# A hybrid decoder layer on one core: a new order for the modulation's weight loads, with the gate rows kept in DRAM

## The reference

```python
mod = silu(c) @ w_ada + b_ada                 # w_ada is 2048 x 12288
sh1, sc1, gt1, sh2, sc2, gt2 = split(mod, 6)
h = rms_norm(x, g_pre_mix) * (1 + sc1) + sh1
u_lru, u_gate, q, k, v, f_logit = split(h @ w_in, ...)
y_lru = rg_lru(conv4(u_lru), ...) * gelu(u_gate)
y_att = fox_attention(q, k, v, cumsum(log_sigmoid(f_logit + b_forget)))     # 8 heads of 128
y = concat(rms_norm(y_lru, g_lru_out), rms_norm(y_att, g_att_out)) @ w_out
x = x + gt1 * rms_norm(y, g_post_mix)
h = rms_norm(x, g_pre_mlp) * (1 + sc2) + sh2
x = x + gt2 * rms_norm(relu(h @ w_ff1) ** 2 @ w_ff2, g_post_mlp)
```

## Time and profile before

| | us |
|---|---|
| median of 3 runs (lowest, highest) | 2317.61 (2315.52, 2321.9) |
| the profiled execution | 2320.91 |
| span of its trace, first to last instruction | 2319.1 |
| PE busy in it | 2150.2 (93%) |
| DVE busy in it | 1627.2 (70%) |
| ACT busy in it | 800.6 (35%) |
| granted TensorE clock, mean | 0.965 of full speed |

### The profile page before, as it was taken

How to read it: one execution, slowest core, us unless ns; L and a number is a source line. 1 busy time by engine, 2 the same in 40 slices (tenths; PEclk the granted TensorE clock), 3 DMA queues, 4 the chain that set the end, 5 groups by cost and what they waited for, 6 DMA issues and landing times.

```text
span 2319.1 us, 25157 instructions
## 1 busy us (share of the span) xinstructions
PE 2150.2 (93%) x9081; PEld 1707.6 (74%) x9081; DVE 1627.2 (70%) x1783; ACT 800.6 (35%) x1032; POOL 159.2 (7%) x140
## 2 busy tenths in 40 slices
PE   4779999999888896699999999999999999999996
PEld 3557778888666675477877877877787787787775
DVE  7998694456774755577677677668668667767756
ACT  4224622222542233234333334333333333333332
POOL 3440040000110001000000000000000000000000
PEclk7789999999999998799999999999999999999998
DMA  9865466647326762433232333232232322323242
GB/s 331 291 223 161 139 193 192 187 121 264 110 87 199 256 207 95 159 101 109 82 118 90 99 99 109 81 118 90 90 112 96 99 99 99 101 89 108 100 150 105
DMA packets 178574, 322.45 MB, mean 139 GB/s; under 512 B 12328, under 2 KB 47256, under 8 KB 176336
## 3 DMA queue, kind: packets, MB, share of 16 engines
q1 hardware_dynamic: 172576, 303.12, 40.3%
q0 software_dynamic: 3680, 17.98, 2.3%
q10 hardware_dynamic: 2256, 0.53, 0.1%
HBM read 313.18 MB, written 8.41 MB: 139 GB/s over the span
## 4 chain that ended last, share of the span: by engine, by line
PE 64%; DVE 19%; issue 8%; ACT 6%; DMA 3%; DVEq 0%; ACTq 0%; SPq 0%
DVE acc L1287 8%; PE pair L749 8%; PE pair L751 8%; PE pair L750 8%; PE pair L773 7%; PE pair L774 6%; PE pair L775 6%; PE bank L462 4%; PE bank L463 4%; PE bank L464 4%; PE bank L472 3%; PE bank L474 3%; PE bank L473 3%; ACT w_hi L1130 2%; DVE w_lo L1542 2%
## 5 line engine op out<-in xcount | busy, mean ns | idle before, releaser
L1620 DVE TENSOR_TENSOR yg<-yg,pair 128x1024 f32<-128x1024 f32 x240 | 289.6, 1217 | 317.0 <-PE pair L775 317.0
L749 PE MATMUL pair<-h_hi,w_lo 128*128 128x512 f32 x1024 | 412.4, 403 | 33.1 <-DVE h_lo L1554 24.1
L751 PE MATMUL pair<-h_hi,w_hi 128*128 128x512 f32 x1024 | 410.4, 401 | 0.0
L750 PE MATMUL pair<-h_lo,w_hi 128*128 128x512 f32 x1024 | 410.3, 401 | 0.0
L773 PE MATMUL pair<-w_hi,op_lo 128*128 128x512 f32 x840 | 333.7, 397 | 3.8 <-DVE op_lo L1587 3.6
L774 PE MATMUL pair<-w_lo,op_hi 128*128 128x512 f32 x840 | 332.8, 396 | 0.0
L775 PE MATMUL pair<-w_hi,op_hi 128*128 128x512 f32 x840 | 331.8, 395 | 0.0
L749 PEld LDWEIGHTS pair<-h_hi,w_lo 128*128 128x128 f32 x1024 | 196.0, 191 | 85.1 <-DVE h_lo L1554 27.2
L1102 ACT ACTIVATE w_hi<-w_raw 128x1024 fp32r<-128x1024 f32 x128 | 135.2, 1056 | 278.5 <-PE pair L751 223.1
L751 PEld LDWEIGHTS pair<-h_hi,w_hi 128*128 128x128 f32 x1024 | 195.9, 191 | 48.2
L750 PEld LDWEIGHTS pair<-h_lo,w_hi 128*128 128x128 f32 x1024 | 196.4, 192 | 47.2
(11 more groups left out here) (252 smaller groups left out, 2884.0 us busy)
## 6 DMA issues: line engine op xcount, KB each, us to landing
raw<-in_w_ada_dram SPq DMA_DIRECT2D x128, 512.0 KB, 4.6
w_raw<-in_w_ff_dram SPq DMA_DIRECT2D x128, 512.0 KB, 3.8
raw<-in_w_ff_dram SPq DMA_DIRECT2D x128, 512.0 KB, 4.5
raw<-in_w_in_dram SPq DMA_DIRECT2D x82, 512.0 KB, 3.8
gst<-in_w_ada_dram SPq DMA_DIRECT2D x64, 512.0 KB, 6.1
raw<-in_w_out_dram SPq DMA_DIRECT2D x32, 512.0 KB, 4.8
x_tok<-in_x_dram SPq DMA_DIRECT2D x4, 1024.0 KB, 8.7
xr<-in_x_dram POOLq DMA_DIRECT2D x4, 1024.0 KB, 7.2
```

Of the source, the lines that this page charges most:

```text
L749: pe.matmul(b, lo[:, cols], h_hi[:, kt, :], start=(kt == 0), stop=False)
L750: pe.matmul(b, hi[:, cols], h_lo[:, kt, :], start=False, stop=False)
L751: last = pe.matmul(b, hi[:, cols], h_hi[:, kt, :], start=False, stop=(kt == KT - 1))
L1620: dve.tensor_tensor(y, y, pairs[2 + (i + r) % 2][:, :, :], ALU.subtract if i == 6 else ALU.add).then_inc(product_read, 1)
```

## The change

- `ada_after` now puts one unit beside every slab from 18 to 113 and one more beside projection slabs e = 20 to 51. That makes 128; none is left for the feed-forward part.
- The PE jobs of groups 0 to 11 stand in the projection (`SUMS_AT`: job by slab e, `SUMS_IN`: its PSUM bank), those of 12 to 14 in the output product (`ROW_AT`), that of 15 in the first chunk of the feed-forward part. The waits ahead of PE's groups of slabs ask for the sums that share their banks.
- Every gate is now one row: DVE multiplies sum and gain into `g_row[0:1]`, POOL stores it to `gate_scr` in DRAM and then loads the next gain (`load_gain`, `store_gate`). `G1` is read back as one broadcast of 1 MB after the last head. The first head's square on ACT waits for four stored gates, because it writes `g_row`.
- SP loads `w_ff1` and the first tiles of `w_ff2` with no unit between them; DVE's loop has no `ada_unit`.

```diff
     def ada_after(n):
-        if U_PROJ <= n < U_ATT:
-            return 1 + (n >= U_ATT - 8)
-        return (U_ATT + 2 <= n < U_OUT + 2) + 2 * (U_OUT + 3 <= n < U_OUT + 19)
+        return (U_PROJ <= n) + (U_PROJ + 20 <= n < U_PROJ + 52)
...
-    COLUMNS_AT = {1: 6, 2: 4, 3: 4, 4: 4, 5: 4, 6: 4, 7: 2}
+    SUMS_AT = {14: 0, 20: 1, 22: 2, 26: 3, 30: 4, 34: 5, 38: 6, 42: 7, 46: 8, 50: 9, 58: 10, 62: 11}
+    SUMS_IN = {0: 0, 1: 4, 2: 5, 3: 0, 4: 1, 5: 4, 6: 5, 7: 0, 8: 1, 9: 1, 10: 5, 11: 7}
...
@@ SP @@
             sp.wait_ge(y_sum, 4)
-            for j in range(8):
-                if j >= 2:
-                    sp.wait_ge(w1_lo, j - 1)
+            load_w1((0, 0), 0)
+            load_w1((0, 0), 1)
+            for which in range(4):
+                raw_done(*stream[-1 - (len(stream) - 1 - which) % RING])
+                load_w2((0, 0), 0, which)
+            for j in range(2, 8):
+                sp.wait_ge(w1_lo, j - 1)
                 load_w1((0, 0), j)
-                for pos in (POS_MLP + 2 * j, POS_MLP + 2 * j + 1):
-                    load(pos)
-            for j in range(2):
-                sp.wait_ge(w1_lo, 7 + j)
-                load_w1((1, 0), j)
-            for which in range(4):
-                sp.wait_ge(ada_used, N_ADA - (len(stream) - 1 - which) % RING)
-                load_w2((0, 0), 0, which)
-            for j in (2, 3):
+            for j in range(4):
                 sp.wait_ge(w1_lo, 7 + j)
                 load_w1((1, 0), j)
...
@@ PE, projection @@
+                taken = sum(at < 8 * gi for at in SUMS_AT)
                 if gi >= 2:
-                    pe.wait_ge(mod_read, 8 + gi - 1)
+                    pe.wait_ge(mod_read, 8 + min(taken, 8))
+                if taken > 8:
+                    pe.wait_ge(gate_ready, taken - 8)
...
-                    if gi and v == COLUMNS_AT[gi]:
+                    if n - U_PROJ in SUMS_AT:
...
-                        column_job(8 + gi - 1, other)
+                        cg = SUMS_AT[n - U_PROJ]
+                        if cg == 11:
+                            pe.wait_ge(gate_ready, 3)
+                        (column_job if cg < 8 else row_job)(8 + cg, banks[SUMS_IN[cg]])
...
-                    if gi == 7 and v == 6:
-                        column_job(8 + 7, banks[7])
...
@@ PE, output product @@
+            SUMS_READ = {1: 5, 3: 6, 5: 7}
+            ROW_AT = {(0, 1): (20, banks[5]), (2, 1): (21, SET_Q[0]), (4, 1): (22, SET_Q[0])}
...
-                if r:
-                    pe.wait_ge(gate_ready, r)
+                if r in SUMS_READ:
+                    pe.wait_ge(gate_ready, SUMS_READ[r])
...
-                        if v == (0, 2, 1, 1, 2)[r]:
+                        if (r, v) in ROW_AT:
...
-                            row_job(16 + r, banks[5] if r == 0 else (SET_Q, SET_P)[r % 2][0])
+                            row_job(*ROW_AT[r, v])
...
                 for t in range(NT):
-                    if t == 1:
-                        pe.wait_ge(half_copied, 16)
-                        row_job(16 + r, SET_P[0])
...
@@ PE, feed-forward part @@
-                if q == 11:
-                    pe.wait_ge(x1t_copied, 4 * NT)
-                    row_job(22, pairs[2][:, 0, :])
-            row_job(23, pairs[3][:, 0, :])
+                if q == 8:
+                    row_job(23, pairs[2][:, 0, :])
...
@@ ACT, first head @@
+                else:
+                    act.wait_ge(gate_stored, 16 * 4)
                 act.activation(g_row[:, :], banks[7][:, :], ACT.Square).then_inc(ya_sq, 1)
...
@@ DVE @@
-                if q < 4:
-                    dve.tensor_tensor(G1[:, q * COLS:(q + 1) * COLS], bank[:, :], g_row[:, :], ALU.mult).then_inc(gate_ready, 1)
...
+                dve.tensor_tensor(g_row[0:1, :], bank[0:1, :], g_row[0:1, :], ALU.mult).then_inc(gate_ready, 1)
...
+                if e - LAG in SUMS_AT:
+                    take_sums(SUMS_AT[e - LAG])
...
-                    for a in (0, 1):
-                        ada_unit(ADA_MLP + kt - 3 + a)
-                if kt == 13:
-                    take_gate(6, pairs[2][:, 0, :])
-            for a in (N_ADA - 2, N_ADA - 1):
-                ada_unit(a)
-            take_gate(7, pairs[3][:, 0, :])
+                if kt == 11:
+                    take_gate(7, pairs[2][:, 0, :])
...
@@ POOL @@
+            load_gain(0)
+            store_gate(0)
+            load_gain(1)
             pool.wait_ge(nf_ready, 1)
...
             mask_nf(0)
+            store_gate(1)
+            load_gain(2)
+            store_gate(2)
+            load_gain(3)
+            store_gate(3)
             for h in range(HEADS):
...
+            pool.wait_ge(att_ssq, HEADS)
+            load_gain(4)
             pool.wait_ge(pv_done, HEADS)
+            pool.dma_start(G1[:, :], gate_scr[0:1, :].to_broadcast([P, D])).then_inc(g1_in, 16)
             load_x(2)
...
```

More of the change, by code:

```diff
@@ L78, in hybrid_layer @@
     POS_MLP = len(stream)
[L79 to L85, removed]
+    assert len(ada_pos) == 16 * 8
     HALVES = KT
@@ L251, in hybrid_layer @@
         y2_zero, unit_done, y2_done = sem("y2_zero"), sem("unit_done"), sem("y2_done")
-        g2_stored, g2_in = sem("g2_stored"), sem("g2_in")
+        gate_stored, g1_in, g2_in = sem("gate_stored"), sem("g1_in"), sem("g2_in")
         x1r_in = sem("x1r_in")
@@ L283, in slot_free, with raw_done @@
                     return
-                kind, n = stream[pos - RING]
+                raw_done(*stream[pos - RING])
+            def raw_done(kind, n):
                 if kind == "ada":
@@ L590, in _ @@
                     bank_of = (SET_Q, SET_P)[gi % 2]
-                    other = (SET_P, SET_Q)[gi % 2][1]
                     if gi == 6:
@@ L644, in weigh_values @@
                     pe.wait_ge(v_copied, 8)
-                    pe.wait_ge(mod_read, 8 + 8)
+                    pe.wait_ge(gate_ready, 4)
                 else:
@@ L728, in _ @@
                     pe.wait_ge(half_copied, 16)
-                    pe.wait_ge(gate_ready, 6)
                 elif t == 1:
@@ L1455, in _ @@
                     forget()
-                for gi in range(1, 8):
-                    if e == 8 * gi + COLUMNS_AT[gi] + LAG:
-                        take_columns(gi - 1, (banks[1] if gi == 6 else banks[5]) if gi >= 6 else banks[(4, 0)[gi % 2]])
+                if e - LAG in SUMS_AT:
+                    take_sums(SUMS_AT[e - LAG])
                 if e == 7 * 8 + 2:
@@ L1490, in gate_y @@
                 dve.wait_ge(y_sq, 4 * [1, 2, 3, 5].index(r) + t + 1)
+                dve.wait_ge(g1_in, 16)
                 dve.tensor_tensor(yg[:, t, cols], yg[:, t, cols], G1[:, cols], ALU.mult).then_inc(y_gated, 1)
@@ L1498, in _ @@
                 if done == 3:
-                    take_gate(0, banks[5])
+                    take_gate(4, banks[5])
                     dve.wait_ge(row_std, 2)
                     step(dve.reciprocal(stat[:, RA:RA + NT], stat[:, RA:RA + NT]))
-                for q, at in ((1, 7), (2, 10), (3, 15), (4, 19)):
+                for q, at in ((5, 11), (6, 19)):
                     if done == at:
-                        take_gate(q, (SET_Q, SET_P)[q % 2][0])
+                        take_gate(q, SET_Q[0])
                 r = done // 4 - 1
@@ L1795, in mask_nf, with load_gain, store_gate @@
                                    causal[:, :].unsqueeze(1).to_broadcast([P, NT, P]), ALU.add).then_inc(nfm_ready, 1)
+            def load_gain(q):
+                if q:
+                    pool.wait_ge(gate_stored, 16 * q)
+                g = (g_post_mix, g_post_mlp)[q // 4]
+                pool.dma_start(g_row[0:1, :], g[0:1, q % 4 * COLS:(q % 4 + 1) * COLS]).then_inc(gain_in, 16)
+            def store_gate(q):
+                pool.wait_ge(gate_ready, q + 1)
+                pool.dma_start(gate_scr[q // 4:q // 4 + 1, q % 4 * COLS:(q % 4 + 1) * COLS], g_row[0:1, :]).then_inc(gate_stored, 16)
+            load_gain(0)
+            store_gate(0)
+            load_gain(1)
             pool.wait_ge(nf_ready, 1)
@@ L1825, in load_x @@
                 pool.dma_start(dst, x2[t * P:(t + 1) * P, :]).then_inc(xr_in[t], 16)
-            load_gain(0)
+            pool.wait_ge(att_ssq, HEADS)
+            load_gain(4)
             pool.wait_ge(pv_done, HEADS)
+            pool.dma_start(G1[:, :], gate_scr[0:1, :].to_broadcast([P, D])).then_inc(g1_in, 16)
             load_x(2)
-            def store_gate2(q):
-                pool.wait_ge(gate_ready, q + 1)
-                pool.dma_start(g2_scr[0:1, (q - 4) * COLS:(q - 3) * COLS], ssq[0:1, :]).then_inc(g2_stored, 16)
-            load_gain(1)
-            load_gain(2)
+            store_gate(4)
+            load_gain(5)
             pool.wait_ge(y_sum, 8)
@@ L1839, in _ @@
             load_x(1)
-            for q in (3, 4, 5):
-                load_gain(q)
-            store_gate2(4)
+            store_gate(5)
+            load_gain(6)
+            store_gate(6)
+            load_gain(7)
             for t in range(NT):
```

(8 more changed lines are left out.)

25 lines of the change are left out of this document (5 added, 20 removed).

## The result

The changed kernel takes 2266.3 us (median of 4 runs, 2262.92 to 2267.88) against 2317.24 (4 runs) for the one before: a ratio of 0.9772, 95% interval 0.976 to 0.9785, so 50.9 us less. Forecast were 2261.2 us in a range of 2250 to 2282. The profiled execution took 2267.88 us with a span of 2265.8, against 2319.1 before: 53.3 us less.

What follows compares the result with a forecast made beforehand. PE, busy 93% of the span, was taken as the bound, so only its waits and slow stretches could give time. Terms -39.5 - 25.1 - 1 + 10.7 - 1.5 = -56.4 us gave 2264.5 profiled, 2261.2 as median; range 2250 to 2282.

Steps and rivals of the forecast that it cites:

- Feed-forward start: First w_ff1 matmul to first product: without units there, a gain of 39.5 us, bounds 33 and 41.
- PE becomes the bound: Feed-forward start: without units DVE needs 3.7 us a pair, ACT under 3, PE 5.63, where a period took 11.3.
- Output product: Its 147.0 us were to become 121.9 without stops for row jobs: gain 25.1 us, bounds 15 and 26.
- A like stop follows some 50 us later: Output product: a second stop like DVE's 13.06 us wait for a row job to free acc, which idles PE 9.69.
- Projection: Double units in slabs 20 to 51 cost 10.7 us: 0.8 late, 8.0 waiting for sum 2, 1.9 restart; bounds 2 and 25.
- The 0.8 ahead of slab 22: Projection: DVE, slowed by GpSimd's squares, splits slab 22 at 336.9 us where PE wants it at 336.1.
- GpSimd's port: Projection, 305 to 333 us: weighings beside GpSimd's work take 1.515 us instead of 0.775; the skill's rule allowed up to 2.55.
- Tiles and x1: Tiles behind the output product: one row job and one gate product go, gain 1 us, bounds 0 and 1.5.
- Attention: Two more units around the first head, but its first slab no longer waits 6.06 us: gain 1.5, bounds -3 and 3.
- The ring ran at PE's pace: Rival, projection: double units go at the output product's 7.0 us a slab, costing 36 us: 2297 us; chance 0.1.
- no gain stayed away: Rival: output product stays at 147 (2286 us), or w_ff1 tiles take 7 us and more a pair (2273); chance 0.15.
- the list in which a `w_in` load is queued behind units did not run in series: Rival, projection: slab loads queued behind units run in series with weighing, 182 us dearer: 2443 us; chance 0.03.

Runs made afterwards that it cites:

- before_reorder: Kernel before, all units kept, each w_ff1 tile's load issued ahead of the units of the tile before it: 2294.8 us, ratio 0.9888.
- first_sum: Changed kernel with double units on slabs 24 to 55, and sum 0 taken one slab behind its job instead of three: 2253.0 us, ratio 0.972.
- before_job_places: Kernel before with the output product's second, third and fourth row jobs each behind the first slab of their group: 2303.1 us, ratio 0.9923.
- early_take: Changed kernel with sums 2, 4, 6 and 8 taken by DVE one slab behind the job instead of three: 2257.2 us, ratio 0.9736.
- no_squares: Changed kernel with GpSimd's squares of channel tiles 4 to 7 and their sums over 8 columns instead of 512: 2262.2 us, one run.
- late_zero: first_sum with GpSimd's memset of y2 cut into four, each behind a split w_ff1 tile: 2248.2 us, ratio 0.9693.

## Why the prediction was right

**Feed-forward start (-39.5, measured -41.2).** The step "PE becomes the bound" held: period 5.62 us for 5.63, one row job, one restart. The sum gave 56.3 us to the first product, the trace 54.6. PE's part came as reckoned (47.6 us for 47.8); from there to the product it takes 7.0 us for 8.5, because the ACT and DVE steps were taken as one after the other and partly overlap. "Loading and DVE's work run one after the other" was right too, and before_reorder gives it a size: at least 25 us of the 40; taking the units away brings the rest. The last two weighings of the changed kernel start at 831.52, so none lies behind 850, as the prediction asked.

**Output product (-25.1, measured -24.9).** The size was right: 122.3 us from its first matmul to the first sum of its last round, for the 121.9 reckoned, at clock 1.00. The reason was right for one stop only. The step that failed is "A like stop follows some 50 us later": its row job can be moved and the idle time stays (7.1 to 7.9 us). In its place the rows point to DVE's load, two units a slab and the work on `y`. The change leaves one unit per slab and no stop, so the sum did not notice; for this stop the right size is luck. `G1`'s broadcast cost nothing: no wait for it is in the trace.

**Projection (+10.7, measured +12.4).** The forecast put DVE's taking of sum 2 at 356.2 us, the trace has its end at 355.9; PE stands there from 348.8 instead of 348.2; the wait was to be 8.0 and is 7.13, the restart 1.9 and is 1.9. The 0.8 ahead of slab 22 did not come: slab 22 was split at 336.1, where 336.9 was reckoned, and PE came to it at 337.0, where 336.1 was reckoned. None of the waits at slabs 32 and 40 came, as held. **The missed term** is four row jobs: the gates' jobs of sums 8 to 11 moved here, two net from the output product, one from the tiles and one from the feed-forward part's start, 0.85 each, 3.4 us. Their going was counted in those three stretches, their coming was not counted here. The prediction's sum for a profiled execution was 2264.5 us; the measured one took 2267.88, 3.4 more. That the two 3.4 agree is partly chance: the other errors of the table, -1.7 to +1.3 each, cancel.

**GpSimd's port.** The forecast took 1.55 us for a weighing beside POOL's additions, near its row's 1.515. The four weighings of slab 21 took 6.37 us, 1.59 each. In that stretch POOL ran squares of 1.31 and additions of 1.61 us or more with gaps of under 0.2, so there was about one weighing to one POOL instruction. The Trainium skill's page SBUF — State Buffer, section "SBUF: two separate sides", from which the prediction had worked out an estimate of up to 2.55 us, says that the later of two such instructions blocks fully. The trace doesn't bear out the price that adds a whole POOL instruction to each weighing; how much of a POOL instruction's recorded time is its own waiting, no run here shows.

**Tiles and x1 (-1, measured 0).** The row job and the gate product went, and in the same place DVE waits 1.36 instead of 0.46 us for ACT's root of the x1 sum. It was cover, not path: the stretch is 41.68 us in both kernels.

**Attention (-1.5, measured -1.6).** Ahead of the second head PE waits 1.61 instead of 4.18 us for DVE's probabilities, in the direction that was forecast. But the agreement to 0.1 is luck. Up to the second head it is 1.0 less and not 2.6, because PE goes on at a granted clock of 0.66 behind its 2.20 us of idling ahead of slab 82, where it was 1.00 behind 2.27 before; the second head gains 2.3 (15.79 to 13.51); and in the later ones two steps of 1.5 stand against one.

**The rest (+1.3)** is clock as well. Windows over 130 us near the end, the same distance behind the first product, before and after:

```profile
2184.36:2314.36 130.00, 113.12 (x476) 90.05 (x474) 84.48 (x93) 43.97 (x70) 2.62 (x5) 0.95 0.34 126
```
```profile
2129.71:2259.71 130.00, 114.42 (x476) 90.98 (x474) 83.53 (x91) 43.78 (x70) 2.65 (x5) 0.94 0.34 126
```

The same 476 matmuls, 1.3 us more of PE. All of it arises behind one wait near the end: over 10 us there the granted clock is 0.83 before (2254.36 to 2264.36) and 0.68 after (2199.71 to 2209.71).

None of the rivals came. The ring ran at PE's pace, no gain stayed away, and the list in which a `w_in` load is queued behind units did not run in series.

## What to carry to other kernels

A stage that asks for a side result should ask for it as late as its own buffers allow, and the engine that makes it should deliver it as soon as it can: here a lead of two slabs was demanded where one was there, and one line gave back 9 us. When work moves, book what comes where it arrives as well as what goes where it leaves; the small fixed jobs that travel with it are easily lost. Before removing work that shares a queue with an urgent load, try the order of the queue: that alone was at least 25 of 40 us. The best version here is the changed kernel with double units from slab 24, sum 0 taken at once and the memset in four pieces behind the first tiles: 2248.2 us.

## What the runs showed of the hardware

- A memset on GpSimd stretched a 0.54 us VectorE instruction to 5.71 us, by 5.2 us where 5.4 of the memset were left. It is one of some 1800 instructions of VectorE and no wait; the timeline shows it.
- After ten idle times from 6.8 to 9.7 us, in five traces, PE's granted clock over the next 5 us was 0.50 to 0.67. After short ones it went either way. Ahead of slab 82 PE idles 2.2 to 2.6 us in all twelve traces, and the next 5 us were at 0.66 to 0.68 in nine of them (the changed kernel too), which costs 1.4 us, and at 1.00 in three (the kernel before, first_sum, before_job_places). The wait of 2.1 us ahead of slab 16 was followed by 0.80 over the next 8.75 us in early_take and by 1.00 in the changed kernel; waits of 2.5 and 3.0 us (no_squares, late_zero) by 1.00. What decides was not found.
- Attention heads with the same work take 13.5 or 15.0 us, at mean clocks of 1.00 and 0.89. What decides between them was not found either, and no run here was made for it.
